# Hybrid decoder step on one core: the units that fill the prompt attention, one a step in three pieces, in six of a pair's eight steps

## The reference, cut to what matters

```python
p = _split_in(jnp.einsum('btd,dn->btn', x, w_in))
logf = jax.nn.log_sigmoid((p['fox_f'] + b_fox_f).astype(jnp.float32))
...
s = jnp.einsum('bqhd,bkhd->bhqk', q_blk, k) * (FOX_HD ** -0.5)
s = s + (jnp.swapaxes(cq_blk, 1, 2)[..., :, None] - ckT[..., None, :])   # c = cumsum(logf)
s = jnp.where(kpos[None, :] <= qpos[:, None], s, -jnp.inf)
p = jax.nn.softmax(s, axis=-1)
return jnp.einsum('bhqk,bkhd->bqhd', p.astype(v.dtype), v)
...
g = jax.nn.sigmoid(p['gate'].reshape(B, T, N_BRANCH, D_MODEL))
```

## Time and profile before

| what | value |
|---|---|
| median of 3 runs | 1741.86 us (1740.83 to 1747.35) |
| the profiled execution, its own time | 1741.02 us |
| its span in the profile | 1739.1 us |
| TensorE busy over the span | 92% |
| mean granted clock of TensorE | 0.966 |

### The profile page before, as it was taken

The page is one execution under the profiler, slowest core; times in us unless marked ns, Lnnn a source line. Parts: engine busy times, 40 slices in busy tenths (PEclk is TensorE's granted clock), DMA queues, the critical chain, the costliest instruction groups (busy, mean ns, idle before and its releaser), DMA issues. The chain is left out here.

```text
span 1739.1 us, 25580 instructions
## 1 busy us (share of the span) xinstructions
PE 1604.4 (92%) x9847; PEld 1468.6 (84%) x9847; DVE 809.4 (47%) x1287; ACT 652.8 (38%) x1101; POOL 249.9 (14%) x312
## 2 busy tenths in 40 slices
PE   7999999999999999999999999999996499999980
PEld 6988788889988888999999999999785388888860
DVE  3433453354033333322033322234633799999965
ACT  4422141212134544422111111123111288888856
POOL 1000111013001211130000000000101135344310
PEclk9999999999999999999999999999997599999995
DMA  6111132124211112052325124112432789999736
GB/s 179 40 37 37 52 111 64 37 64 159 68 56 41 59 49 77 19 171 84 117 77 176 50 61 139 37 37 104 147 126 70 246 251 277 324 301 290 180 60 223
DMA packets 154225, 204.34 MB, mean 117 GB/s; under 512 B 14724, under 2 KB 121236, under 8 KB 154105
## 3 DMA queue, kind: packets, MB, share of 16 engines
q1 hardware_dynamic: 132472, 130.86, 24.3%
q0 software_dynamic: 21632, 71.85, 14.5%
HBM read 152.34 MB, written 50.34 MB: 117 GB/s over the span
## 5 line engine op out<-in xcount | busy, mean ns | idle before, releaser
L382 PE MATMUL ps<-xh,slab_hi 128*128 128x384 f32 (+1 forms) x504 | 173.0, 343 | 2.3 <-DVE xl L741 2.3
L382 PE MATMUL ps<-xl,slab_hi 128*128 128x384 f32 (+1 forms) x504 | 166.6, 331 | 0.0
L382 PE MATMUL ps<-xh,slab_lo 128*128 128x384 f32 (+1 forms) x504 | 166.6, 330 | 0.0
L1882 PE MATMUL ps<-xh,slab_lo 128*128 128x384 f32 (+1 forms) x384 | 125.2, 326 | 0.0
L1882 PE MATMUL ps<-xh,slab_hi 128*128 128x384 f32 (+1 forms) x384 | 125.2, 326 | 0.0
L1882 PE MATMUL ps<-xl,slab_hi 128*128 128x384 f32 (+1 forms) x384 | 125.2, 326 | 0.0
L2083 DVE TENSOR_TENSOR gt_sg<-ps,gt_sg 128x384 f32<-128x384 f32 (+1 forms) x48 | 25.7, 536 | 186.5 <-PE ps L1882 186.3
L382 PEld LDWEIGHTS ps<-xh,slab_hi 128*128 128x128 f32 x504 | 96.1, 191 | 16.5 <-issue 12.0
L2746 PE MATMUL ps<-mo_hi_gu,mo_xh 128*128 128x512 f32 x256 | 100.9, 394 | 0.0
L2746 PE MATMUL ps<-mo_hi_gu,mo_xl 128*128 128x512 f32 x256 | 100.8, 394 | 0.0
L382 PEld LDWEIGHTS ps<-xh,slab_lo 128*128 128x128 f32 x504 | 96.3, 191 | 0.0
(11 more groups left out here) (458 smaller groups left out, 4141.0 us busy)
## 6 DMA issues: line engine op xcount, KB each, us to landing
slab_raw<-in_w_in SPq DMA_DIRECT2D x60, 512.0 KB, 4.1
mo_raw_g<-in_w_e_gate SPq DMA_DIRECT2D x16, 1024.0 KB, 8.8
mo_raw_u<-in_w_e_up SPq DMA_DIRECT2D x16, 1024.0 KB, 14.0
mo_raw_d<-in_w_e_down SPq DMA_DIRECT2D x16, 1024.0 KB, 7.4
gt_oh<-oT_hi SPq DMA_DIRECT2D x3, 2176.0 KB, 8.0
gt_ol<-oT_lo SPq DMA_DIRECT2D x3, 2176.0 KB, 12.8
slab_raw<-in_w_branch SPq DMA_DIRECT2D x24, 256.0 KB, 4.9
x_dram<-slab_raw POOLq DMA_DIRECT2D x9, 512.0 KB, 5.2
```

Of the source, the lines that this page charges most:

```text
L382: mm = eng.matmul(out, w[:, b, k, :], x[:, k, t0:t0 + tn], start=(k == 0 and j == 0), stop=(k == KC - 1 and j == 2), skip_group_check=True)
L1882: last = eng.matmul(out, w[:, s % 2, c, wk, :], x[:, k, t0:t0 + tn], start=(k == 0 and i == 0), stop=(k == ks[-1] and i == 2))
```

## The change

A unit is cut in three pieces of 3, 3 and 2 chunks (9, 9 and 6 matmuls) in place of four of 2 chunks (6 matmuls each). The three places for a piece in a step stay where they are. Before, the 24 pieces of a pair went over the 24 places of its eight steps, so a unit began and ended at changing places: the six ends lay in step 1 at the first place, step 2 at the second, step 3 at the third, step 5 at the first, step 6 at the second and step 7 at the third. Now unit u takes the three places of step u, and steps 6 and 7 have no piece. `place_unit` and `tail_unit` stand once a step, at the place at which the third stood. The same holds for the gate units of pair 3.

```diff
+        THIRDS = ((0, 3), (3, 6), (6, KC))
...
             def piece(Q, i):
-                p, j = Q // 8 + 1, 3 * (Q % 8) + i
-                u, part = divmod(j, 4)
+                p, u = Q // 8 + 1, Q % 8
+                k0, k1 = THIRDS[i]
+                if u >= 6:
+                    return
                 if p < 4:
-                    project(p, u // 3, u % 3, 2 * part, 2 * part + 2)
+                    project(p, u // 3, u % 3, k0, k1)
                     return
-                if j == 0:
+                if (u, i) == (0, 0):
                     eng.wait_ge(unit_free, kq_unit(3, 1, 2) + 1)
                     eng.wait_ge(sh.g_split, 1)
-                elif part == 0:
+                elif i == 0:
                     eng.wait_ge(sh.sg_ready, u)
-                mm = gate_quarter(sh, eng, sh.ps[:, 0, :], u, part)
-                if part == 3:
+                mm = gate_chunks(sh, eng, sh.ps[:, 0, :], u, k0, k1)
+                if i == 2:
                     mm.then_inc(sh.gate_mm, 1)
...
-            def place_unit(Q, i):
-                p, j = Q // 8 + 1, 3 * (Q % 8) + i
-                if p < 4 and j % 4 == 3:
-                    (place_keys if j < 12 else place_queries)(p, j // 4 % 3)
-                elif p == 4 and j % 4 == 3:
-                    place_gate(j // 4)
+            def place_unit(Q):
+                p, u = Q // 8 + 1, Q % 8
+                if u < 6 and p < 4:
+                    (place_keys if u < 3 else place_queries)(p, u % 3)
+                elif u < 6:
+                    place_gate(u)
...
             for Q in range(NQ):
-                place_unit(Q, 0)
                 place_probs(Q, 0)
...
-                place_unit(Q, 1)
                 place_probs(Q, 1)
...
                 if Q + 1 < NQ:
                     exponent(Q + 1, 1)
-                place_unit(Q, 2)
+                place_unit(Q)
```

More of the change, by code:

```diff
@@ L1463, in query_tails, with tail_unit @@
                                          in1=f32(qh[:, t0:t0 + pn]), op0=ALU.mult, op1=ALU.subtract).then_inc(unit_free, 1)
[L1465 to L1468, removed]
+            def tail_unit(Q):
+                p, u = Q // 8 + 1, Q % 8
+                if u < 6 and p < 4:
+                    (key_tails if u < 3 else query_tails)(p, u % 3)
             def lowest(Q, h):
@@ L1510, in _ @@
                     lowest(Q + 1, 0)
-                tail_unit(Q, 0)
                 if Q + 1 < NQ:
@@ L1515, in _ @@
                     out_tail(Q - 1)
-                tail_unit(Q, 1)
-                tail_unit(Q, 2)
+                tail_unit(Q)
                 if Q < 24 and Q % 8 == 1:
@@ L1586, in gate_quarter, with gate_chunks @@
 def gate_quarter(sh, eng, bank, u, part):
+    return gate_chunks(sh, eng, bank, u, 2 * part, 2 * part + 2)
+def gate_chunks(sh, eng, bank, u, k0, k1):
     _raw, hi, lo = weight_views(sh, 2, 12)
     s, c, (t0, tn) = u // 6, u % 6 // 3, GROUPS[u % 3]
-    for k in (2 * part, 2 * part + 1):
+    for k in range(k0, k1):
         for i, (w, x) in enumerate(((hi, sh.xh), (hi, sh.xl), (lo, sh.xh))):
```

## The result

The changed kernel takes 1758.47 us (median of 5 runs, 1753.68 to 1761.86), against 1741.86 before. The ratio is 1.0093 with a 95% interval of 1.0073 to 1.0112, so it is slower by 0.9%. The profiled execution took 1758.47, its span is 1756.8, 17.7 more than before.

What follows compares the result with a forecast made beforehand. PE was taken as the bound. New stalls of 15.4 + 3.4 + 0.9 less 12.7 removed gave +7.0, the clock +4.5, so +11.5: median 1753.4 us from 1741.86; range 1740 to 1763.

Steps and rivals of the forecast that it cites:

- The forecast's own narrower range: Whole kernel: range of the main forecast alone, 1749 to 1758 us; chance 0.48.
- What is removed: PE's filler-unit boundary waits: 12.7 us go, 0.9 us stays behind step 0.
- the case without a hold-up: Rival, step 6: work behind the queries' wait is hidden, costing 6.4 us; -2.0 in all, 1739.9 us; chance 0.12.
- Step 6: PE stalls behind the ACT and DVE chain: 5.2, 5.2, 3.4 and 1.6 us in pairs 0 to 3, 15.4 in all.
- The hold-up's share in the sum: Step 6: part of its 15.4 us due to query copies waiting for step 7's scores, beyond 4 x 1.6; 9.0 us.
- Step 7: PE stalls of 0.6, 0.6, 1.9 and 0.3 us in pairs 0 to 3, 3.4 in all.
- The clock: Thin step 6 of pairs 0 to 2 lowers PE's clock: 1.5 us three times, 4.5 (bounds nothing to 13.6).
- The rival with a slow clock in all eight steps: Steps 6 and 7 of all pairs: 13.6 us for the clock plus 7.0, 1762.5 us; chance 0.09.
- the moved filler: Loop: boundary waits removed against stalls in steps 6, 7 and behind step 0, without hold-up or clock; -2.0 us.

Runs made afterwards that it cites:

- the kernel with both edits: Changed kernel with query group 2 read out in step 6, not 5, and useless matmuls (12 and 0 in step 6, 8 and 6 in step 7): 1740.45 us.
- the two runs with added matmuls: Changed kernel with useless matmuls in steps 6 and 7, all waits kept: 1750.07 us; similar, with query group 2 also read out in step 6: 1740.45 us.
- the later read-out: Changed kernel with query group 2 read out at the end of step 6 instead of step 5, PE's program the same: 1738.45 us.

## Why the prediction was right, and where it was off

The direction held, 1758.5 lies in the stated range, and the forecast of 1753.4 is 5 us low. The forecast's own narrower range ended at 1758. In the loop the miss is larger: it grew by 18.5 us, where the sum had 11.5.

**What is removed** was sized right. The boundary waits went from 12.7 us to 0.7 against 0.9 forecast. In the kernel with both edits, the loop is 1.0 us shorter than before, where the case without a hold-up said 2.0, and some 2 us of added matmuls are still in it. The medians of the two kernels can't tell this gain from nothing.

**Step 6** was right in its chain. The values began 6.7 us after the scores in pair 1 (forecast 6.9), 4.9 in pair 2 (5.05) and 3.35 in pair 3 (3.3). The wait before the output's transpose was 2.48 (2.6). The wait before the values was 1.41 and not 2.6, because the half clock stretched the transposes ahead of it from 0.93 to 1.69 us. The hold-up's share in the sum, 15.4 - 4 x 1.6 = 9.0, stands against about 7.0 at a full clock, from the two runs with added matmuls. In pairs 0 and 1 it is 3.3 us each (forecast 3.6), so most of the difference is in pair 2, where the kernel with both edits has a wait of 0.8 us of its own in step 7.

**Step 7** had no large waits in the profile after. The forecast's 1.5 us in pair 2 did not come, since the slow values of step 6 gave ACT and DVE time. With step 6 at full clock, in the run with added matmuls in step 6 alone, it did show there, as 0.5.

**The clock** is the term that was mis-sized: 4.5 us forecast, 9.8 measured net of the added matmuls, and about 12.4 without them. I took one slow stretch of 3.5 us, as at the front, in three pairs. There were four stretches, of 13, 13, 10 and 7 us. The price by time was right where PE set the pace (6.24 us for 3.23 us of work), the duration was not. The clock fell without any long stand of PE: its longest wait there was 2.48 us, and it worked for 0.72, 0.79 and 1.06 us in the three windows from 622 to 628 us. That much the forecast had right. How long the clock stays down it took from the front, and there it failed. The rival with a slow clock in all eight steps was nearer in kind, but at 1.7 us a step it reached 1762.5 with the waits beside it, which a slower PE partly covers.

So the sum that explains the loop's 18.5 us is: -1.0 for the moved filler, +7.0 for the hold-up, +12.4 for the clock. The forecast had -2.0, +9.0 and +4.5. With the matmuls of step 7 taken out as well, an estimate, the first term is nearer to -3 and the last nearer to 14. The hold-up was too high by 2 us and the clock too low by 8. The errors partly cancel, so that the total of 11.5 stands nearer to 18.5 than the clock's term to its measured size, and that much is luck.

The last two terms are not independent. With the hold-up, keeping the clock was worth 9.8 us net, without it 2.4; and taking the hold-up away was worth 17.1 us where the clock was free to fall, about 7.0 where it was kept. The sum holds for the profiled executions. By the medians, each against the kernel before beside it, the same three steps are -0.3, +9.6 and +7.3, where the profiles have -1.0, +9.6 and +9.8, all with the added matmuls in them. The changed kernel's runs differ by up to 8 us and I profiled one. Their mean granted clocks go from 0.957 in the fastest to 0.952 in the slowest, so the time at the lower clock differs from run to run; in which stretches is open.

## What to carry to other kernels

When work is moved to make room at one wait, look up what its consumers wait for themselves: here a copy that was ready two steps sooner found its target still in use, and everything queued behind it on two in-order engines was late. A rebalancing should keep filler in the steps with the longest dependent chains, since what it covers is not only the waits but also the clock. Two profiles in which an engine stands still for the same time can differ by what its clock costs: look at the granted clock and at the busy time of the same instructions. And when matmuls of no use are added as a probe, check in every pair that they are hidden: here they were in two of four.

## What was unexpected of the hardware

Once down, the clock stayed at 0.50 while PE was recorded as busy without a gap. In the changed kernel the window from 636 to 638 us has PE busy for 2.00 of 2.00 us and 0.50, and from 630 on every window was as full, with the values of step 6 and the short scores and transposes of step 7. At the front, the clock was back after about 3 us. What makes the difference was not tried.

Nearly equal stretches had different ends. With the later read-out, PE was busy for 1.07 of 2 us at 550 and the clock fell, in the next pair for 1.17 of 2 us at 616 and it did not. The runs with added matmuls show the same in a stricter form: the same matmuls, placed alike to 0.01 us, kept the clock in one execution and lost it in the other. A thin stretch of this size is a risk to the clock and not a fixed price.
